# Splitting the first weight tile inside three attentions and rounding their last output chunk in the stage that follows

## Time and profile before

| | us |
|---|---|
| three runs | 3252.75, 3256.26, 3259.72 (median 3256.26) |
| the profiled execution | 3251.75 |
| its span, first to last instruction | 3250.0 |
| `at` of layer 0 and of layer 1, `gqa`: from first peaks to last product with v | 246.6 to 374.8, 1036.0 to 1163.6, 2534.1 to 2644.0 |
| TensorE busy | 3107.6 (96%) |
| VectorE, ScalarE, GpSimd busy | 1560.5 (48%), 1049.9 (32%), 238.0 (7%) |

### The profile page before, as it was taken

One profiled execution on the slowest core, in us unless ns is written; L12 is line 12 of the kernel. 1 busy time (PEld: TensorE's weight loads), 2 busy tenths in 40 slices (PEclk: granted clock), 3 DMA queues, 4 the chain that ended last, 5 costly groups with the idle time before them and its releaser, 6 DMA issues. The chain is left out here.

```text
span 3250.0 us, 39838 instructions
## 1 busy us (share of the span) xinstructions
PE 3107.6 (96%) x15942; PEld 2119.3 (65%) x15942; DVE 1560.5 (48%) x2099; ACT 1049.9 (32%) x1661; POOL 238.0 (7%) x363
## 2 busy tenths in 40 slices
PE   8999999999999999999998999999989899999996
PEld 6886688888787568888885574454437457454442
DVE  5315558888522565888856461211126656121113
ACT  4325434444323634444443422000013543200002
POOL 1004200000101510000010200000000320000000
PEclk9999999999999999999998999999998999999999
DMA  6410133331441022333302138999992124999997
GB/s 178 128 41 27 65 104 104 104 102 60 129 132 37 1 91 91 104 104 104 99 28 68 52 152 368 421 414 422 422 381 66 59 65 176 375 421 413 422 422 311
DMA packets 229162, 590.38 MB, mean 182 GB/s; under 512 B 37814, under 2 KB 141180, under 8 KB 179852
## 3 DMA queue, kind: packets, MB, share of 16 engines
q1 hardware_dynamic: 229004, 588.16, 48.1%
HBM read 581.82 MB, written 2.10 MB: 180 GB/s over the span
## 5 line engine op out<-in xcount | busy, mean ns | idle before, releaser
L3066 PE MATMUL ps<-w_ring,xe 128*64 128x512 f32 x1024 | 229.4, 594 | 7.0 <-DMA w_ring<-in_w 4.8
L3066 PE MATMUL ps<-ex_front,xe 128*64 128x512 f32 x1024 | 232.9, 598 | 0.0
L3066 PE MATMUL ps<-ex_front,hidT 128*64 128x512 f32 x1024 | 225.8, 597 | 4.7 <-DMA ex_front<-in_w 2.4
L1147 ACT ACTIVATE mlp_w_hi<-w_ring 128x2048 fp32r<-128x2048 f32 x86 | 165.3, 1926 | 185.7 <-PE ps L1084 69.9
L1249 DVE TENSOR_TENSOR mlp_w_lo<-w_ring,mlp_w_hi 128x2048 fp32r<-128x2048 f32 x86 | 196.5, 2287 | 46.1 <-ACT mlp_w_hi L1147 46.1
L361 PE MATMUL ps<-h_hi,in_w_hi 128*128 128x512 f32 (+1 forms) x528 | 207.1, 392 | 0.2 <-DVE h_lo L439 0.2
L361 PE MATMUL ps<-h_lo,in_w_hi 128*128 128x512 f32 (+1 forms) x528 | 205.7, 390 | 0.0
L361 PE MATMUL ps<-h_hi,in_w_lo 128*128 128x512 f32 (+1 forms) x528 | 205.6, 389 | 0.0
L1084 PE MATMUL ps<-h_hi,mlp_w_hi 128*128 128x512 f32 x512 | 199.8, 390 | 0.6 <-DVE h_lo L1355 0.4
L1084 PE MATMUL ps<-h_hi,mlp_w_lo 128*128 128x512 f32 x512 | 199.3, 389 | 0.0
L1084 PE MATMUL ps<-h_lo,mlp_w_hi 128*128 128x512 f32 x512 | 199.2, 389 | 0.0
(11 more groups left out here) (613 smaller groups left out, 6505.9 us busy)
## 6 DMA issues: line engine op xcount, KB each, us to landing
ex_front<-in_w SPq DMA_DIRECT2D x256, 1024.0 KB, 14.9
w_ring<-in_w SPq DMA_DIRECT2D x128, 1024.0 KB, 16.7
w_ring<-in_w_in SPq DMA_DIRECT2D x32, 1024.0 KB, 5.4
w_ring<-in_w_up SPq DMA_DIRECT2D x32, 1024.0 KB, 9.2
w_ring<-in_w_down SPq DMA_DIRECT2D x32, 1024.0 KB, 5.2
w_ring<-in_cmp_w SPq DMA_DIRECT2D x16, 512.0 KB, 4.7
w_ring<-in_w_out SPq DMA_DIRECT2D x8, 1024.0 KB, 6.0
w_ring<-in_w_o SPq DMA_DIRECT2D x8, 1024.0 KB, 8.9
```

Source lines behind the costliest of these rows:

```text
L1147: act.activation(w.hi[:, number(m, n) % HOMES, :], src, ACT.Copy).then_inc(s.hi_done, 1)
L3066: mm = pe.matmul(ps[rows, bank + half, :], lhsT, slot(2 * m + a)[:, kk, 512 * half:512 * half + 512], start=(k == 0), stop=(k == DC - 1))
```

## The change

`attention` gets `begin`, a pair of tensors. In the two `at` and in `gqa`, ScalarE and VectorE split the first weight tile of the next stage, which lies in ring slot 0, in four pieces of 128 x 512, at the steps nu*(n+1)//5: 9, 19, 28 and 38 in `at`, 6, 12, 19 and 25 in `gqa`. ScalarE's piece comes after the exponentials of the step; VectorE's comes after its peaks and reciprocals and ahead of its copy of unit s-3, and waits for ScalarE's piece of the same step. The `keep` of the last chunk is taken out of the attention; the next stage runs it first on ScalarE and VectorE (`carry`), and TensorE waits for it ahead of the second tile. The next stage does not split its first tile (`begun`): TensorE starts on it with no wait. The tensors are the first home of the split tiles in the stages `in`, `wy` and `w_o1`. `mla` is called as before.

```diff
-def gemm(..., banks=NB, kept=None):
+def gemm(..., banks=NB, kept=None, begun=False, carry=None):
...
-        parts = min(4, first)
-        cuts = [first * q // parts for q in range(parts + 1)]
+        parts = 0 if begun else min(4, first)
+        cuts = [first] if begun else [first * q // parts for q in range(parts + 1)]
...
                     if n >= RING:
-                        sp.wait_ge(s.split, splits(n - RING))
+                        if splits(n - RING):
+                            sp.wait_ge(s.split, splits(n - RING))
...
                     for o in outs_of[n]:
+                        if carry and k == last[0]:
+                            pe.wait_ge(s.carried, 1)
...
                 def split(n):
-                    if n >= n_w:
+                    if n >= n_w or n == 0 and begun:
                         return
...
+                if carry:
+                    carry.hi(act).then_inc(s.carried_hi, 1)
                 split(0)
...
+                if carry:
+                    dve.wait_ge(s.carried_hi, 1)
+                    carry.lo(dve).then_inc(s.carried, 1)
                 split(0)
...
-def attention(nc, label, ps, C, groups, kind, oT, ring, nxt, cmp=None, scratch=None):
+def attention(nc, label, ps, C, groups, kind, oT, ring, nxt, cmp=None, scratch=None, begin=None):
...
+    BEGIN_PARTS = 4
+    begin_at = [(n + 1) * nu // (BEGIN_PARTS + 1) for n in range(BEGIN_PARTS)] if begin else []
+    last_group = len(groups) - 1 if begin else len(groups)
+    begin_ready = ring.sets[ring.now][0]
...
                 def keep(g):
-                    if closes(g):
+                    if closes(g) and g < last_group:
...
                     if step < nu:
                         exponentials(step)
+                    if step in begin_at:
+                        cols, q = begin_part(step)
+                        act.wait_ge(begin_ready, 16)
+                        act.activation(begin.hi[:, cols], ring.slots[:, 0, cols], ACT.Copy).then_inc(s.begun_hi, 1)
...
                     if 1 <= step <= nu:
                         inverses(step - 1)
+                    if step in begin_at:
+                        cols, q = begin_part(step)
+                        dve.wait_ge(s.begun_hi, q)
+                        dve.tensor_tensor(begin.lo[:, cols], ring.slots[:, 0, cols], begin.hi[:, cols].bitcast(F32), ALU.subtract).then_inc(s.begun_lo, 1)
...
+    if begin:
+        c, b = groups[-1].chunk, bank_of(len(groups) - 1)
+        return Names(hi=lambda act: act.activation(oT.hi[:, c, :], ps[:, b, :], ACT.Copy),
+                     lo=lambda dve: dve.tensor_tensor(oT.lo[:, c, :], ps[:, b, :], oT.hi[:, c, :].bitcast(F32), ALU.subtract))
...
-            gemm(nc, "wy", ps, ring, y_tiles + w_out, 2, first_ups(I["w_up"][l]))
+            gemm(nc, "wy", ps, ring, y_tiles + w_out, 2, first_ups(I["w_up"][l]), kept=y_begun, begun=True, carry=carry)
```

More of the change, by code:

```diff
@@ L222, with gemm @@
 IDLE_PASSES = 12
-def gemm(nc, label, ps, ring, tiles, pre=0, nxt=(), lead=None, also=(), side=None, banks=NB, kept=None):
+def gemm(nc, label, ps, ring, tiles, pre=0, nxt=(), lead=None, also=(), side=None, banks=NB, kept=None, begun=False, carry=None):
     rms = lead.rms if lead else None
@@ L265, in gemm @@
         first = tiles[0].kc if n_w and not tiles[0].raw else 1
-        parts = min(4, first)
-        cuts = [first * q // parts for q in range(parts + 1)]
+        assert not (begun and lead)
+        parts = 0 if begun else min(4, first)
+        cuts = [first] if begun else [first * q // parts for q in range(parts + 1)]
         def splits(n):
@@ L279, in gemm @@
         before = [max((j for j in range(k) if bank[j] == bank[k] and (outs[j].a or outs[j].v)), default=None) for k in range(len(outs))]
-        names = "out_done hi_done split evac_a evac_v chain_a chain_v also flipped lead_hi lead_done"
+        names = "out_done hi_done split evac_a evac_v chain_a chain_v also flipped lead_hi lead_done carried_hi carried"
         with stage(nc, label, f"{names} {side.names}" if side else names, clear=ready) as (block, s):
@@ L325, in _ @@
                 for n, t in enumerate(tiles):
-                    if 0 < n < n_w or n < n_w and len(outs_of[0][0].mm) // 3 != first:
+                    if 0 < n < n_w or n < n_w and not begun and len(outs_of[0][0].mm) // 3 != first:
                         pe.wait_ge(s.split, splits(n))
@@ L571, in attention, with begin_part @@
     mixed_by = [sum(TT + p for p in pieces[:g + 1]) for g in range(len(groups))]
+    BEGIN_PARTS = 4
+    def begin_part(step):
+        q = [(n + 1) * nu // (BEGIN_PARTS + 1) for n in range(BEGIN_PARTS)].index(step)
+        return slice(q * SLOT // BEGIN_PARTS, (q + 1) * SLOT // BEGIN_PARTS), q + 1
+    begin_at = [(n + 1) * nu // (BEGIN_PARTS + 1) for n in range(BEGIN_PARTS)] if begin else []
+    last_group = len(groups) - 1 if begin else len(groups)
+    begin_ready = ring.sets[ring.now][0]
     with ExitStack() as ctx:
@@ L584, in attention @@
         names = "scored peaked maxed exped inverse normed flipped copied_a copied_v mixed o_hi o_done"
+        if begin:
+            names += " begun_hi begun_lo"
         if cmp:
@@ L832, in _ @@
                         take(step - LAG)
+    if begin:
+        c, b = groups[-1].chunk, bank_of(len(groups) - 1)
+        return Names(hi=lambda act: act.activation(oT.hi[:, c, :], ps[:, b, :], ACT.Copy),
+                     lo=lambda dve: dve.tensor_tensor(oT.lo[:, c, :], ps[:, b, :], oT.hi[:, c, :].bitcast(F32), ALU.subtract))
+    return None
 def log_sigmoid(act, dve_ready, act_chain, z, t):
@@ L856, in block1_layer @@
         y_tiles, mixed_of, oT_of = mix_tiles(I, l, sga, sgb)
+        y_begun = pair(nc, ctx, "y_begun", [P, SLOT])
         with ExitStack() as c2:
@@ L913, in block1_layer @@
                 with nc.allow_non_contiguous_dma("narrow columns"):
-                    gemm(nc, "in", ps, ring, tiles, pre, lead=lead, side=side, banks=PREP_BANKS)
+                    gemm(nc, "in", ps, ring, tiles, pre, lead=lead, side=side, banks=PREP_BANKS, kept=y_begun)
             with ExitStack() as c3:
@@ L933, in block1_layer @@
                             gate=g[:, :, 0:24:3].rearrange("q i (r a) -> q a i r", a=2))
-                attention(nc, "at", ps, C, groups, "causal", h, ring, y_tiles, cmp, kvc)
+                carry = attention(nc, "at", ps, C, groups, "causal", h, ring, y_tiles, cmp, kvc, begin=y_begun)
         with ExitStack() as c2:
@@ L2431, in odd_tiles, with odd_mixer @@
     return [tile(DC, 256, lambda slot, c=c: [(slot, W(w_in, DC, c, 256))], None) for c in (1024, 0, 256, 512)]
-def odd_mixer(nc, ps, ring, C, I, x, mixT, nxt):
+def odd_mixer(nc, ps, ring, C, I, x, mixT, nxt, begin):
     w_in = I["w_in_odd_2"][0]
@@ L2468, in odd_mixer @@
                         sharp=lambda i, c=c: rq[:, i, 2 * c:2 * c + 2]) for c in range(8)]
-        attention(nc, "gqa", ps, C, groups, "full", mixT, ring, nxt)
+        return attention(nc, "gqa", ps, C, groups, "full", mixT, ring, nxt, begin=begin)
 HEAD_BANKS = 4
@@ L3265, in block2_layer @@
             allot(nc, ctx, mixT, f"mixT{i}", [P, DC, T])
-            odd_mixer(nc, ps, ring, C, I, x, mixT, w_o)
-            lead = None
+            begun, lead = pair(nc, ctx, "w_o_begun", [P, SLOT]), None
+            carry = odd_mixer(nc, ps, ring, C, I, x, mixT, w_o, begun)
         else:
@@ L3270, in block2_layer @@
             even_mixer(nc, ctx, ps, ring, C, I, x, mixT, og, w_o)
+            begun = carry = None
             lead = flips(C, lambda i, j: og[:, i, j * P:(j + 1) * P], mixT[:, 4:8, :], 4)
-        gemm(nc, f"w_o{i}", ps, ring, w_o, RING, ple, lead, side=layer_norm_beside(nc, ctx, C, x, I["ln1_g_2"][i], I["ln1_b_2"][i], f"ln1{i}"))
+        gemm(nc, f"w_o{i}", ps, ring, w_o, RING, ple, lead, side=layer_norm_beside(nc, ctx, C, x, I["ln1_g_2"][i], I["ln1_b_2"][i], f"ln1{i}"),
+             kept=begun, begun=begun is not None, carry=carry)
     with ExitStack() as ctx:
```

## The result

The changed kernel takes 3273.0 us (median of 10 runs, 3264.9 to 3290.7) against 3260.1 us of the kernel before (median of 10, 3249.1 to 3267.6). The ratio is 1.0050 with a 95% interval of 1.0035 to 1.0065: slower, by about 16 us (11.4 to 21.2; the medians alone differ by 12.9), where I forecast slower by 7.9. One of the ten runs, the one of 3290.7 us, shows a mean clock of 0.935 where the others show 0.979 to 0.982; without it the highest is 3276.2. The profiled execution took 3273.78 us, its span is 3271.9.

A forecast was written before the change was run, and what follows sets the result against it. TensorE, busy 96% of the span, was taken as the bound; -12.9 (boundaries) + 17.2 (inner waits) + 3.6 (clock) = +7.9 us on the median 3256.26, giving 3264.2 us. Stated range 3250 to 3274; the forecast's own 3257 to 3271.

The forecast's parts named there:

- Boundary: At the three attention ends: gap from 3.06 to 0.32 us and clock staying up, 12.9 us gained together.
- The waits inside: In the attention loops: pieces delay copies TensorE waits for; gqa 7.4, each at 4.9, together 17.2 us.
- The clock inside: Inside the attentions: six new waits, three falls of the clock at 1.2 us each, 3.6 us; bounds 0 and 9.6.
- Theory C: In the first follow-up's expectations: inner waits as forecast, clock falls an accident of one execution; +17, 3277.
- Two signs of the prediction: gqa takes 7 to 10 us more than 109.9; VectorE idles over 2 us at pieces in the named steps.
- Rival 3: Inside the attentions: all six waits lose the clock, 9.6 in place of 3.6; +13.9 us, 3270.2; chance 0.08.
- Rival 2: Behind the two dear steps of each attention: loops take up the delays, faster; -10 us, 3246; chance 0.12.
- rival 1: Inside the attentions: the clock stays up in the new waits; +4.3 us, 3260.6; chance 0.22.
- rival 4: At the boundaries: the clock falls as before, 4.7 us of gain missing; +12.6 us, 3268.9; chance 0.05.
- Rival 5: In the attentions: pieces and GpSimd scalings meet, 1.3 us for each of 12 pieces; +23.5 us, 3279.8; chance 0.03.

The follow-up runs named there:

- Experiment 4: Changed kernel with all four pieces moved behind the last copy of each attention; 3244.7 us, ratio 0.9962 to the kernel before.
- experiment 5: Changed kernel with the scores of a later unit computed two extra times in the six long TensorE waits; 3259.4 us, ratio 1.0011 to the kernel before.
- experiment 1: Changed kernel with attention end and next stage as in the kernel before, pieces still split inside; 3284.4 us, ratio 1.0078 to the kernel before.
- experiment 6: Changed kernel with all four pieces of each attention in steps where the copy is VectorE's own; 3287.8 us, ratio 1.0098 to the kernel before.
- experiment 7: Kernel before with only the last chunk's rounding moved into the next stage, no pieces in the attention; 3250.3 us, ratio 0.9984 to the kernel before.
- experiment 3: Changed kernel with the pieces moved to steps where the copy is ScalarE's; 3256.0 us, ratio 0.9998 to the kernel before.

## Why the prediction was half right

**Boundary: right.** 0.32 us of gap and a clock that stays up, as in the earlier trace rows; 13.2 us in the traces, forecast 12.9. Experiment 4 has this gain alone: 12.4 us by the ratio (interval 7.8 to 17).

**The waits inside: right.** The place, the order that makes them and their size. By the run with filled waits (us, forecast in brackets): `at` steps 9 and 28, 0.26 and 0.48 (0.3 each); 19, 2.51 (2.3); 38, 2.00 (2.0); `gqa` steps 6 and 19, 2.85 and 2.80 (2.8); 12 and 25, 1.00 and 0.85 (0.9). Sum over the three attentions 18.0, forecast 17.2.

**The clock inside: this term was mis-sized.** I took "three falls of 1.2 us", 3.6 us. In the profile of the changed kernel the clock fell behind five of the six long waits. Four of the five stretches lasted 6.8 us, from 351.4 to 358.2 for instance, and they cost 2.75 and 2.95 us (`at`, layer 0), 2.69 (layer 1) and 2.74 (`gqa`); the short one cost 0.82. This is changed kernel less filled waits, in the table: 12.0 us together. Two errors lie in it: I counted a fall as one stretch of the length of the earlier trace rows, and took half of the waits, though the earlier trace rows showed a fall with 2.05 us and all six new waits were as long or longer. The trace of before could have corrected the first: the fall of the earlier trace rows itself lasted 6.8 us, from 255.9 to 262.7. My upper bound, 6 x 1.6 = 9.6, was too low as well. With the measured term the sum is -12.9 + 18.0 + 12.0 = 17.1 us; measured are 16.3 (11.4 to 21.2). So the step of the prediction that failed is this term: five falls that cost 12.0 us, not three that cost 3.6. Theory C, that the falls were an accident of one execution, is refuted by experiment 5: were it so, filling the waits would have changed the times hardly at all, and over twelve runs it saved 12.7 us.

Two signs of the prediction show the same: `gqa` takes 12.8 us more (forecast 7 to 10), 1.7 of it ahead of its first piece; VectorE idles 2.13 to 2.14 us at the pieces of `gqa` but 1.75 to 1.96 at the two dear ones of each `at` (forecast over 2). That the 3273.0 us lie inside the stated 3250 to 3274 is no support: the forecast's own range ended at +14, which takes the upper bound for the clock but not the one for the waits; both together give -12.9 + 21 + 9.6 = +17.7.

**The rivals.** Rival 3, all waits lose the clock, was the nearest in kind, with its price too low. Rival 2 (the loops take up the delays) and rival 1 (the clock stays up) did not happen, nor did rival 4 (the clock falls at the boundaries as before). Rival 5 happened in a small way: I had costed the meeting of a piece with GpSimd's scaling at nothing, arguing from the order at step 19. At step 28 of both `at` they do meet (changed kernel, layer 0):

```profile
323.21 1.52 POOL L785 TENSOR_SCALAR w_ring<-w_ring,at_inv,g 128x512 f32<-128x512 f32 x2 [0.30 <-DVE at_inv L807]
324.24 1.02 DVE L838 TENSOR_TENSOR y_begun_lo<-w_ring,y_begun_hi 128x512 fp32r<-128x512 f32 x1 [1.13 <-ACT y_begun_hi L764]
```

The piece takes 1.02 us in place of 0.69, since GpSimd is at its second scaling until 324.73. That is 0.33 us, twice in the kernel. The Trainium skill ("SBUF — State Buffer", "SBUF: two separate sides") states that the one that starts first holds the shared ports and the other stands still. The trace agrees in who is slowed; standing still until 324.73 would be 0.49 us, measured are 0.33. GpSimd's scalings are not slowed here (busy 48.7 us in `gqa` and 115 us in the two `at`, as before).

## What to carry to other kernels

Work put "beside" a loop on idle engines is priced by what is queued behind its waits, not by its duration: ask on which engine the next thing that the bound engine needs is queued, and give a two-engine hand-over a step in between. The same pieces cost 30 us, 9 us, 2 us or nothing, by their place. And if this kernel's own trace shows the clock falling behind waits of TensorE of some length, price such a wait at nearly twice its length: here six waits of 2.15 to 2.77 us cost another 12.0 us, 2 us each on average, four of them 2.7 to 3.0, one 0.8 and one nothing.

## What was not expected

- Behind the five, four and seven falls inside the attentions of the changed kernel and experiments 1 and 6, the clock was at 1.2 GHz for 6.8 us in four, three and three cases, and for 3.4 us in the others. At the boundaries, with the gaps of 3.06 and 2.27 us (the kernel before and experiments 1 and 7), it was 3.4 us in all falls but one. The products after an inner wait come with more waits between them; I did not test that this is the reason.
- Two extra products of the scores for each head in each of six waits, some 12 us of added work for TensorE, made the kernel 13 to 14 us faster than the changed one.
- The length of a wait does not settle whether the clock falls. At step 38 of the changed kernel 2.15 us were followed by a fall in layer 0 and by none in layer 1; in experiment 1 the 3.35 us at step 6 of `gqa` were not followed by one; and an early wait of 1.73 us in `gqa` was followed by one in the changed kernel and in experiments 1, 3 and 7, but not in the kernel before. What does settle it stays open. Whether these falls make up the spread between runs was not shown either: with the waits filled the times still spread over 9 us.
